# Attention of a streaming encoder on TensorE: sample values of both heads in one product, narrow products spread, key sums on VectorE and key roots on GpSimd

## The reference, cut to what matters

```python
att = MLA(c_q, c_kv, k_rot)   # 16 heads x 64 values, query and key of 64 + 32 (rotary), QK-norm
# per head: q = rms_norm(c_q @ w_uq), k = rms_norm([c_kv @ w_uk | k_rot]), v = c_kv @ w_uv
s = einsum('bqhd,bkhd->bhqk', q, k) * QK_DIM ** -0.5      # QK_DIM = 96
p = softmax(where(visible, s, -inf));  out = einsum('bhqk,bkhd->bqhd', p, v)
```

## Time and profile before

| | us |
|---|---|
| median of 3 runs | 3242.81 (3238.13 to 3245.23) |
| profiled execution | 3247.03, span 3245.3 |
| TensorE busy | 2862.5 |
| VectorE busy | 2019.5 |
| ScalarE busy | 1380.2 |
| GpSimd busy | 315.7 |
| mean granted TensorE clock | 0.91 |

### The profile page before, as it was taken

The page is one execution under the profiler, slowest core; times in us unless marked ns, Lnnn a source line. Parts: engine busy times, 40 slices in busy tenths (PEclk is TensorE's granted clock), DMA queues, the critical chain, the costliest instruction groups (busy, mean ns, idle before and its releaser), DMA issues.

```text
span 3245.3 us, 43898 instructions
## 1 busy us (share of the span) xinstructions
PE 2862.5 (88%) x18152; PEld 2624.5 (81%) x18152; DVE 2019.5 (62%) x3294; ACT 1380.2 (43%) x1938; POOL 315.7 (10%) x457
## 2 busy tenths in 40 slices
PE   2998789999798999999789969998888969999996
PEld 2988678888787999999789958887877958888884
DVE  4666666664554443434577567665545368988997
ACT  1334156553333221212333336654333347777773
POOL 3000023330000000000000023221000010000001
PEclk9999789887788999999899979888879889999998
DMA  4322200002131222222122210001212179999995
GB/s 134 124 66 65 56 17 17 9 26 68 65 104 65 65 79 79 78 79 78 59 65 66 65 28 21 11 1 67 91 63 94 66 278 381 384 386 392 384 380 190
DMA packets 219143, 385.28 MB, mean 119 GB/s; under 512 B 34486, under 2 KB 156406, under 8 KB 218944
## 3 DMA queue, kind: packets, MB, share of 16 engines
q1 hardware_dynamic: 202640, 329.80, 28.7%
q0 software_dynamic: 16304, 52.66, 4.6%
HBM read 352.99 MB, written 29.44 MB: 118 GB/s over the span
## 4 chain that ended last, share of the span: by engine, by line
PE 69%; DVE 19%; ACT 8%; issue 2%; DMA 1%; POOL 1%; DVEq 0%; ACTq 0%; POOLq 0%
PE ACC L433 19%; PE ACC L435 18%; PE ACC L434 18%; PE TP L433 3%; PE TP L434 2%; PE TP L435 2%; DVE TR L1574 2%; DVE WL L1363 2%; DVE XC L1541 1%; ACT P L1139 1%; PE TP L905 1%; PE TP L607 1%; DVE PTL L1391 1%; PE ACC L627 1%; PE TP L616 1%
## 5 line engine op out<-in xcount | busy, mean ns | idle before, releaser
L433 PE MATMUL ACC<-XH,WH 128*128 128x288 f32 x1984 | 595.7, 300 | 40.0 <-DVE XP L1442 36.7
L435 PE MATMUL ACC<-XH,WL 128*128 128x288 f32 x1984 | 596.2, 301 | 0.0
L434 PE MATMUL ACC<-XL,WH 128*128 128x288 f32 x1984 | 594.8, 300 | 0.0
L2040 DVE TENSOR_TENSOR WL<-MW,WH 128x2048 fp32r<-128x2048 f32 x192 | 436.9, 2289 | 76.6 <-ACT WH L1297 76.6
L958 ACT ACTIVATE WH<-RAW 128x2048 fp32r<-128x2048 f32 (+1 forms) x129 | 238.0, 1845 | 523.5 <-PE ACC L435 515.5
L1297 ACT ACTIVATE WH<-MW 128x2048 fp32r<-128x2048 f32 x192 | 368.0, 1918 | 145.4 <-PE ACC L435 93.1
L433 PEld LDWEIGHTS ACC<-XH,WH 128*128 128x128 f32 x1984 | 381.0, 192 | 43.4 <-DVE WL L1363 43.1
L434 PEld LDWEIGHTS ACC<-XL,WH 128*128 128x128 f32 x1984 | 380.9, 192 | 0.0
L435 PEld LDWEIGHTS ACC<-XH,WL 128*128 128x128 f32 x1984 | 379.4, 191 | 0.0
L1363 DVE TENSOR_TENSOR WL<-RAW,WH 128x2048 fp32r<-128x2048 f32 (+1 forms) x129 | 284.0, 2202 | 103.0 <-ACT WH L958 102.5
L433 PE MATMUL ACC<-YH,WH 128*128 128x288 f32 x864 | 260.5, 302 | 28.1 <-DVE YL L1914 14.5
(11 more groups left out here) (488 smaller groups left out, 6429.6 us busy)
## 6 DMA issues: line engine op xcount, KB each, us to landing
MW<-in_moe_w_dram SPq DMA_DIRECT2D x192, 1024.0 KB, 7.2
RAW<-in_w_in_dram SPq DMA_DIRECT2D x36, 1024.0 KB
RAW<-in_ffn_w_dram SPq DMA_DIRECT2D x30, 1024.0 KB
dispatched<-ZT POOLq DMA_DIRECT2D x4, 2048.0 KB, 17.8
RAW<-in_w_out_dram SPq DMA_DIRECT2D x8, 1024.0 KB
RAW<-in_w_mk_dram SPq DMA_DIRECT2D x8, 1024.0 KB
RAW<-in_w_mv_dram SPq DMA_DIRECT2D x8, 1024.0 KB
RAW<-in_w_mq_dram SPq DMA_DIRECT2D x8, 1024.0 KB
```

The lines of the kernel that those rows point to most:

```text
L433: nc.tensor.matmul(out, a[0], b[0], start=first, stop=False)
L434: nc.tensor.matmul(out, a[0], b[1], start=False, stop=False)
L435: return nc.tensor.matmul(out, a[1], b[0], start=False, stop=last)
L2040: v.tensor_tensor(low, MW[raw_place(PLACE[key])][:].rearrange("p j n -> p (j n)"), high.bitcast(F32), ALU.subtract)\
```

## The change

- `weighted_values` keeps only the prompt's 12 products. The samples' probabilities of both heads stand side by side (PSH, PSL: 128 columns), and `sample_values` multiplies them with the values of both heads by 15 products a pair, after the odd head's prompt values. Each head uses its own half of the result (`sample_output`, two VectorE operations after one wait).
- `query_squares` takes one head: ten products, each in its own bank. The squares of the even head come after the even head's values, those of the odd head after the turned keys.
- The third group of keys and values and the next even head's queries come before the probabilities of the even head are turned; the next odd head's queries are cut in two halves, ahead of and behind the turn of the odd head's probabilities.
- The key squares are summed by one VectorE `tensor_reduce` (`key_sums`); the roots go to GpSimd, in 15 small steps ahead of the key products.
- ScalarE and VectorE orders follow. The weight split for the pair after next moves: on ScalarE ahead of the odd head's softmax, on VectorE between the even head's output and the odd head's division.
- PSL and QSQ1 get other addresses in the two layers, and `query_scales` is parted in `query_means` (one a head) and the roots.

```diff
 def attention_order():
-    b = [("qs", 0)] + [("kt", 0, n) for n in range(3)]
+    b = [("qs", 0), ("qs", 1)] + [("kt", 0, n) for n in range(3)]
         a += [("s01", even), ("s23", even)]
-        a += [("kv", p + 1, g) for g in range(3)] if more else []
+        a += [("kv", p + 1, g) for g in range(3)] + [("q", even + 2)] if more else []
         a += [("s01", odd), ("s23", odd)]
-        a += [("q", even + 2), ("q", odd + 2)] if more else []
+        a += [("q", odd + 2)] if more else []
         b += [("kt", odd, n) for n in range(3)]
-        b += [("t", even, n) for n in range(4)] + [("pv", even, n) for n in range(2)]
+        b += [("t", even, n) for n in range(4)] + [("pv", even)]
+        b += [("qs", even + 2)] if more else []
         b += [("t", odd, n) for n in range(4)]
-        b += [("qs", p + 1)] + [("kt", even + 2, n) for n in range(3)] if more else []
-        b += [("pv", odd, n) for n in range(2)]
+        b += [("kt", even + 2, n) for n in range(3)] + [("qs", odd + 2)] if more else []
+        b += [("pv", odd), ("pvs", p)]
...
+                def sample_values(pair):
+                    emptied_b(*(("t", 2 * pair + j, 1) for j in range(2)))
+                    bank = bank_b(("pvs", pair))
                     for k in (1, 2, 3, 4, 0):
                         n = rows(k + 4)
-                        mm = product(bank[:, 0:NEW], tuple(v[0:n, k + 4, :, :].rearrange("p a b -> p (a b)") for v in (VH, VL)),
-                                     (PSH[0:n, k, :], PSL[0:n, k, :]), k == 1, k == 0)
+                        mm = product(bank[:, 0:2 * NEW], tuple(v[0:n, k + 4, :, :].rearrange("p a b -> p (a b)") for v in (VH, VL)),
+                                     (PSH[0:n, k, :], PSLS[layer][0:n, k, :]), k == 1, k == 0)
...
                     if more:
                         wq, wkv = attention_weights()
-                        keys_and_values(wkv, p + 1, (0, 1))
+                        keys_and_values(wkv, p + 1, (0, 1, 2))
+                        queries(wq, even + 2)
                     turn_first(even)
                     turn_second(even)
-                    if more:
-                        keys_and_values(wkv, p + 1, (2,))
                     scores(odd)
                     weighted_values(even)
                     if more:
-                        queries(wq, even + 2)
+                        query_squares(even + 2)
+                        bank = bank_a(("q", odd + 2))
+                        query_half(wq, odd + 2, bank, 0)
                     turn_first(odd)
                     turn_second(odd)
                     if more:
-                        queries(wq, odd + 2)
-                        query_squares(p + 1)
+                        query_half(wq, odd + 2, bank, 1).then_inc(s["a_ready"], 1)
                         turn_keys(even + 2)
+                        query_squares(odd + 2)
                     weighted_values(odd)
+                    sample_values(p)
...
                     softmax(even)
+                    keys_high(odd)
+                    divided(even)
                     if p:
                         mixed_high(p - 1)
-                    divided(even)
-                    keys_high(odd)
                     if more:
-                        keys_out(p + 1, 0)
-                    if p + 2 < PAIRS:
-                        split_high(UA)
-                    if more:
-                        keys_out(p + 1, 1)
+                        for g in range(3):
+                            keys_out(p + 1, g)
+                        keys_squared(p + 1)
+                        queries_squared(even + 2)
                     first_high(even)
                     second_high(even)
                     if more:
-                        keys_out(p + 1, 2)
-                        keys_squared(p + 1)
+                        queries_high(even + 2)
+                    if p + 2 < PAIRS:
+                        split_high(UA)
                     softmax(odd)
                     divided(odd)
-                    if more:
-                        queries_squared(even + 2)
-                        queries_high(even + 2)
...
+                def key_sums(pair):
+                    n = 2 * KT
+                    dve.wait_ge(s["k_sq"], layer * PAIRS + pair + 1)
+                    if pair:
+                        dve.wait_ge(s["ka"], layer * PAIRS + pair)
+                    v.tensor_reduce(RK[:, 0, 0:n], KA[:, :, :, 0:NOPE].rearrange("p t h n -> p (t h) n"), AX_X, ALU.add)\
+                        .then_inc(s["k_sum"], 1)
...
                     divide_first(even)
                     reciprocals_second(even)
+                    keys_low(odd)
                     if p:
                         mixed_low(p - 1)
-                    keys_low(odd)
+                    if more:
+                        key_sums(p + 1)
+                        queries_scaled(even + 2)
                     first_low(even)
+                    second_low(even)
+                    if more:
+                        queries_low(even + 2)
+                    maxima(odd)
+                    head_output(even)
                     if p + 2 < PAIRS:
                         split_low(UA)
-                    second_low(even)
-                    maxima(odd)
                     divide_first(odd)
                     reciprocals_second(odd)
                     if more:
-                        key_roots()
-                    head_output(even)
-                    if more:
-                        queries_scaled(even + 2)
-                        queries_low(even + 2)
+                        query_means(even + 2)
                     first_low(odd)
                     second_low(odd)
                     if more:
                         queries_scaled(odd + 2)
                         queries_low(odd + 2)
-                        query_scales(p + 1)
                         keys_low(even + 2)
+                        query_means(odd + 2)
+                        query_scales()
                     head_output(odd)
+                    sample_output(p)
...
+                def assemble_keys(pair):
+                    n, half, y = 2 * KT, ROPE // 2, RK[:, 2, 0:2 * KT]
+                    v, x, q = nc.gpsimd, RK[:, 0, 0:n], RK[:, 1, 0:n]
+                    pool.wait_ge(s["k_sum"], layer * PAIRS + pair + 1)
                     both = x.rearrange("p (t h) -> p t h", h=2)
+                    step(v.tensor_tensor(both, both, krs[:, :].unsqueeze(2).to_broadcast([P, KT, 2]), ALU.add))
+                    step(v.tensor_scalar(x, x, 1.0 / QK, EPS, ALU.mult, ALU.add))
+                    step(v.tensor_scalar(y.bitcast(I32), x.bitcast(I32), -0.5, 1597463007.0, ALU.mult, ALU.add))
+                    for _ in range(3):
+                        step(v.tensor_tensor(q, x, y, ALU.mult))
+                        step(v.tensor_tensor(q, q, y, ALU.mult))
+                        step(v.tensor_scalar(q, q, -0.5, 1.5, ALU.mult, ALU.add))
+                        step(v.tensor_tensor(y, q, y, ALU.mult))
```

More of the change, by code:

```diff
@@ L314, in stream_step_kernel @@
         KTH, KTL = put("KTH", [P, KEYS], F32R), put("KTL", [P, KEYS], F32R)
-        QSQ = [put("QSQ0", [P, T]), at("QSQ1", [P, T], F32, WL0 - 4 * (UNIT - UA))]
+        QSQ0 = put("QSQ0", [P, T])
+        QSQS = [(QSQ0, slot_end("QSQ1%d" % k, [P, T], F32, 1 - k)) for k in range(DEPTH)]
         AO = put("AO", [P, T])
@@ L609, in turn_keys, with query_squares @@
                         mm.then_inc(s["b_ready"], 1)
-                def query_squares(pair):
-                    bank = bank_b(("qs", pair))
-                    for j in range(2):
-                        pe.wait_ge(s["q_sq"], layer * N_HEADS + 2 * pair + j + 1)
-                        for tt in range(TT):
-                            mm = nc.tensor.matmul(bank[0:rows(tt), j * TT + tt:j * TT + tt + 1], QSQ[j][0:QK, tt * P:tt * P + rows(tt)],
-                                                  ones[0:QK, 0:1], start=True, stop=True)
+                def query_squares(head):
+                    bank = bank_b(("qs", head))
+                    pe.wait_ge(s["q_sq"], layer * N_HEADS + head + 1)
+                    for tt in range(TT):
+                        mm = nc.tensor.matmul(bank[0:rows(tt), tt:tt + 1], QSQS[layer][head % 2][0:QK, tt * P:tt * P + rows(tt)],
+                                              ones[0:QK, 0:1], start=True, stop=True)
                     mm.then_inc(s["b_ready"], 1)
@@ L667, in weighted_values @@
                         pe.wait_ge(s["v_lo"], layer * PAIRS + head // 2 + 1)
-                    emptied_b(*(("t", head, n) for n in range(4)))
-                    bank = bank_b(("pv", head, 0))
+                    emptied_b(*(("t", head, n) for n in (0, 2, 3)))
+                    bank = bank_b(("pv", head))
                     for j in range(4):
@@ L1066, in values_high @@
                     if pair:
```

(18 more changed lines are left out.)

89 lines of the change are left out of this document (40 added, 49 removed).

## The result

Four runs of the changed kernel have a median of **3298.48 us** (3287.61 to 3304.47), against 3244.02 (3238.13 to 3251.13) for the kernel before on the same chips. The ratio is **1.0163, 95% interval 1.0129 to 1.0197**: slower by 54 us, where I forecast 9 us faster, and outside my range. The profiled execution took 3297.97 for a span of 3296.3.

What follows compares the result with a forecast made beforehand. TensorE was taken to bound the attention stage, part of its work at half clock. Waits +10, layer starts -5.6, contention +2 and clock -16 sum to -9.6, said as -9: median 3234 us, range 3226 to 3242.

Steps and rivals of the forecast that it cites:

- Step 1: Sample values: 15 products of 128 columns at 0.127 us each replace 30; work per pair falls 1.9, to about 34.8.
- Step 2: Query squares: 20 products of 2.34 us become two runs of ten, 1.14 each, no work saved.
- Step 3: TensorE's new waits: 4.9 us instead of 2.3, full-clock pair 39.7 against 39.03, +10 us over 14 pairs.
- (b): Before the odd head's values, for the PSUM bank of the first turned keys: wait 1.4 us, where it was 0.80.
- (c): Before the query products, for ScalarE's emptying of the second keys-and-values group: wait 0.7 us.
- (d): Before the first keys-and-values group the wait of 1.05 us stays; the 0.43 goes with the key roots.
- (a): Before the turn of the odd head's probabilities, VectorE being late: wait 1.4 us, then 0.3 for the second part.
- Step 4: Key sums on VectorE, roots on GpSimd: layer start 2.8 us shorter, -5.6 in all; steady pairs hide the steps.
- Step 5: VectorE and GpSimd contention, weight split beside key products: 0.15 us a pair, +2; bounds 0 and 1.16 (+16).
- Step 6: TensorE's clock: one 3.4 us fall a pair instead of about 2.4 falls, 4.3 slow microseconds fewer; -16 us, bounds 0 and -25.
- slower, by the waits: Rival: idle time at the odd head's turn and the bank behind it lowers the clock; 3249 to 3269, taken 3255; chance 0.24.

Runs made afterwards that it cites:

- both_moved: Changed kernel, weight split behind odd head's division, next turned keys drained ahead of odd head's queries, that head's squares after its values; 3211.5 us, 0.9881 of the kernel before.
- query_whole: both_moved with both halves of the odd head's queries ahead of the turn of its probabilities; 3206.8 us, 0.9873 of the kernel before.
- samples_alone: Kernel before with both heads' sample values in one product at the pair's end, no engine's other steps moved; 3227.0 us, 0.9949 of the kernel before.
- split_later: Changed kernel with VectorE's weight split behind the odd head's division and reciprocals; 3253.1 us, 1.0034 of the kernel before.
- split_early: Kernel before with VectorE's weight split moved between the odd head's maxima and division, where the change puts it; 3251.1 us, 1.0008 of the kernel before.
- start_roots: samples_alone with VectorE's key reduction and GpSimd's roots in the first pair of each layer only; 3223.5 us, 0.9921 of the kernel before.
- roots_back: Changed kernel with key sums halved on GpSimd and key roots on VectorE again, as in the kernel before; 3350.2 us, 1.0340 of the kernel before.
- keys_first: Changed kernel with next pair's turned keys drained ahead of odd head's queries, that head's squares after its values, split unmoved; 3281.4 us, 1.0107 of the kernel before.
- samples_twice: query_whole with the sample values head by head again, 30 products of 64 columns instead of 15; 3270.0 us, 1.0074 of the kernel before.
- scales_late: samples_alone with the turned keys' split on VectorE ahead of the roots of the query scales; 3228.5 us, 0.9928 of the kernel before.
- output_later: both_moved with the even head's output behind the odd head's division, ahead of its reciprocals; 3234.4 us, 0.9956 of the kernel before.

## Why the prediction was wrong

**Step 1, sample values: the size right, the gain of another kind.** 1.93 for fifteen products, as taken. The busy time of a full-clock pair fell by less, from 36.74 to between 35.2 and 35.5 (both_moved, query_whole, samples_alone), not to 34.8. In the old order waits eat all of it, and the 15.5 us come with the clock; in query_whole's order the merge is worth 63 us.

**Step 2, squares: right.** Ten squares take 1.21 in two places, where I had 1.14 (query_whole's and the change's timelines alike), and nothing is saved.

**Step 3, the waits: places right, one size wrong.** (b) up to 1.64 for 1.4, (c) 0.60 for 0.7, (d) 1.05 as said, in seven pairs of twelve, (a) 1.6 to 2.4 for 1.4 where there is a split. With the largest of each this is 34.8 + 6.1 = 40.9 instead of 39.03, at most +26 over 14 pairs in place of +10. split_later shows that the split ahead of the division is needed for the long wait; split_early shows that it is not enough without the new order. That the lost cover of 2.4 is the part of the new order that matters is still argued.

**Step 4, roots: nearly right in the change, wrong elsewhere.** The reduction took 1.35, the steps 0.21 to 0.23; the start gained 1.9 a layer of 2.8 (start_roots -3.5 us). Among GpSimd's steps one now and then takes 0.6 to 0.95; that is part of the difference.

**Step 5, contention: the mis-sized term of the waits.** I priced 0.15 a pair with an upper bound of 1.16. By roots_back against the change it is 0.8 on average over the pairs with a split, and 1.5 in four of ten. I had the row that warned of it, and gave it a price as if it could fall anywhere; it falls in the one chain that TensorE waits for. (I also misread that row: the 1.74 stands beside GpSimd's low part of the values, 1.80 long, not beside the keys; beside the key products the same small steps take 0.36 to 1.09.) The rule of the Trainium skill (SBUF — State Buffer, "SBUF: two separate sides"), that a VectorE operation with two SBUF inputs and a GpSimd one exclude each other, agrees with the trace in its direction: the key product beside the weight split took 3.07 instead of 1.16, 1.9 more for a split of 1.47, and in another pair 1.72 instead of 0.43, 1.3 more.

**Step 6, the clock: the step that failed.** I expected 4.3 slow microseconds fewer a pair and -16 us. (8.0 less one fall of 3.4 would be 4.6; the slip is worth 1 us.) There are 5.0 more (12.94 for 7.97). What I left out stood in my own rival: a wait ahead of the narrow turns counts with them. In the profiled executions the slow microseconds follow the work and the gaps together:

- the long wait before the turn (1.6 to 2.4): 12.9 and 12.3 with it (the change, keys_first), 6.3 and 5.4 without (split_later, both_moved);
- 0.78 among the turns: 5.4 to 7.4;
- the wait before the turn gone, waits left only before wide products: 1.1 (query_whole);
- 15 narrow products more and no new wait: 8.8 (samples_twice).

The loss is 4.35 a pair. The profile has it as 3.76 more idle time and 0.59 more busy time, though the merged products take 1.3 to 1.9 of work away; so the lower clock added 1.9 to 2.5 of work. An estimate by step 3 parts it alike: at most 40.9 - 39.0 = 1.9 would be waits at full clock, the remaining 2.5 clock. No pair of the change ran at full clock, so the parting is not measured. The rival "slower, by the waits" named the place and the condition (slow time a pair does not drop by 2 of its 8), and priced it at 3255: it let the falls stay, and they grew.

What stays open is the rule by which the clock falls: scales_late gained slow time by losing a wait, two pairs of output_later kept 1.00 with two waits at the turns, and both_moved's pairs, with equal work, lie between 1.00 and 0.87. Nor was the change tried with key products that avoid VectorE's division, so its share in the slow microseconds is not known apart from the wait.

## What to carry to other kernels

Before a step is moved on one engine, look at what covers it on the other: the weight split was free in the old order, where a whole query product stood before the turn, and the halved product left waits of only 0.3 to 0.5 without the split. Where waits can't be avoided, try to have them ahead of wide products and not ahead of a run of transposes: here 1.4 us less of wait before the turn was worth 3.5 to 4.0 a pair. That is what this kernel shows, not a rule. And price VectorE and GpSimd on the same tiles where they meet, in the chain that is waited for.

## What the runs showed of the hardware

- The granted clock fell to 0.50 within a wait of 2 us with TensorE idle, and equally behind 3.9 us of 64-column products with TensorE 100% busy. The Trainium skill (TensorE: Matmul & The Clock Gate, "Loop structure matters more than you think") blames waits between products; the trace agrees for the one (the change, 12.9 slow microseconds), not for the other (samples_twice, 8.8, with no wait beside the slow stretch shown).
- A product of 64 and one of 128 columns both take 0.13 us at full clock, so merging two is worth one of them, and in query_whole's order about as much again in clock: 63 us for 30 us of products.
- Beside GpSimd's key products an addition of 64x1 on VectorE took 1.03 us instead of 0.13 and the pair of divisions 0.94 instead of 0.55, and a GpSimd product beside a VectorE split 3.07 instead of 1.16. How much is lost depends on which GpSimd product the split meets: the chain from split to last division took 2.8 with GpSimd idle, and 3.0, 3.4 or 4.3 beside it.
